# Latent attention's products split into high and low fp32r parts, with its heads prepared at other steps

## What is computed

```
proj = h @ w_in
q_g, k_g, v_g, q_lat, kv_lat = split(proj)
...
c_q = rms_norm(q_lat, mla_q_norm)
q_m = (c_q @ w_q_b).reshape(B, S, 8, 96)
q_m = concat([q_m[..., :64], apply_rope(q_m[..., 64:])])
c_kv = rms_norm(kv_lat[..., :128], mla_kv_norm)
k_rope = apply_rope(kv_lat[..., 128:])
kv = (c_kv @ w_kv_b).reshape(B, S, 8, 128)
k_m = concat([kv[..., :64], k_rope for every head])
v_m = kv[..., 64:]
o_m = blocked_attention(q_m, k_m, v_m, 96 ** -0.5)
merged = concat([rms_norm(o_g), rms_norm(o_m)])
return merged @ w_o
```

## Time and profile before

| | |
|---|---|
| median of 3 runs | 3003.57 us (3002.53 to 3005.95) |
| profiled execution, span from first to last instruction | 3003.8 us (no other time of it is shown) |
| TensorE matmul busy | 2816.4 us (94%) |
| VectorE busy | 1422.1 us (47%) |
| ScalarE busy | 1129.1 us (38%) |
| GpSimd busy | 238.4 us (8%) |
| chain that ended last | PE 82%, DVE 7%, DMA 4%, ACT 4% |

### The profile page before, as it was taken

How to read it: one execution, slowest core, us unless ns; L and a number is a source line. 1 busy time by engine, 2 the same in 40 slices (tenths; PEclk the granted TensorE clock), 3 DMA queues, 4 the chain that set the end, 5 groups by cost and what they waited for, 6 DMA issues and landing times.

```text
span 3003.8 us, 40104 instructions
## 1 busy us (share of the span) xinstructions
PE 2816.4 (94%) x16212; PEld 2094.2 (70%) x16212; DVE 1422.1 (47%) x2150; ACT 1129.1 (38%) x1920; POOL 238.4 (8%) x229
## 2 busy tenths in 40 slices
PE   7999979989999979999999789999999999799998
PEld 5657854536658745447877578888888787578886
DVE  6665532237666333244555763333334654753444
ACT  4664431124665321135233652222222542643332
POOL 0011020000011110001011010000001111000001
PEclk9999989999999989999999899999999999999999
DMA  4011249981002259993435122223320234222220
GB/s 157 29 43 59 86 173 415 415 366 64 29 29 100 100 237 418 414 395 127 144 115 153 40 76 113 112 114 128 124 84 16 88 122 130 81 84 99 98 99 28
DMA packets 67909, 428.28 MB, mean 143 GB/s; under 512 B 7968, under 2 KB 8352, under 8 KB 20368
## 3 DMA queue, kind: packets, MB, share of 16 engines
q1 hardware_dynamic: 62144, 407.96, 35.6%
q0 software_dynamic: 4432, 15.67, 1.6%
q10 hardware_dynamic: 1152, 2.10, 0.2%
HBM read 416.78 MB, written 8.91 MB: 142 GB/s over the span
## 4 chain that ended last, share of the span: by engine, by line
PE 82%; DVE 7%; DMA 4%; ACT 4%; issue 2%; POOL 2%; SPq 0%; DVEq 0%; ACTq 0%; POOLq 0%
PE banks L854 78%; PE banks L855 4%; DMA weight<-in_w_up 3%; ACT arena L1685 3%; DVE arena L2390 3%; POOL arena L3200 2%; DVE arena L3046 1%; DVE arena L2679 0%; DVE weight_part L2494 0%; DMA block_tokens_high<-df_stage 0%; DVE arena L2677 0%; DMA weight<-in_ada_w 0%; ACT weight_part L1685 0%; DVE x L2390 0%; POOL block_tokens_low L3214 0%
## 5 line engine op out<-in xcount | busy, mean ns | idle before, releaser
L1685 ACT ACTIVATE arena<-banks 128x512 f32<-128x512 f32 (+2 forms) x513 | 281.2, 550 | 885.0 <-PE banks L854 779.4
L854 PE MATMUL banks<-weight,arena 128*64 128x512 f32 (+4 forms) x2136 | 429.1, 573 | 21.3 <-DMA weight<-in_w_up 9.2
L854 PE MATMUL banks<-hidden,weight_part 128*128 128x512 f32 (+1 forms) x2304 | 446.8, 355 | 0.0
L854 PEld LDWEIGHTS banks<-hidden,weight_part 128*128 128x128 f32 x2304 | 381.2, 189 | 70.4 <-issue 3.8
L854 PE MATMUL banks<-tokens_high,weight_part 128*128 128x512 f32 (+1 forms) x1536 | 409.0, 357 | 10.0 <-ACT tokens_high L1685 10.0
L2494 DVE TENSOR_TENSOR weight_part<-weight,weight_part 128x2048 fp32r<-128x2048 f32 x124 | 285.8, 2308 | 194.8 <-ACT weight_part L1685 194.7
L1685 ACT ACTIVATE weight_part<-weight 128x2048 fp32r<-128x2048 f32 x124 | 236.4, 1908 | 349.7 <-PE banks L854 336.4
L854 PEld LDWEIGHTS banks<-weight,arena 128*64 128x64 f32 (+2 forms) x2136 | 150.9, 135 | 255.4 <-issue 233.8
L854 PEld LDWEIGHTS banks<-tokens_high,weight_part 128*128 128x128 f32 x1536 | 273.9, 190 | 62.5 <-DVE arena L2390 16.0
L3200 POOL TENSOR_TENSOR arena<-arena 128x512 f32<-128x512 f32 (+1 forms) x89 | 116.0, 1303 | 1974.3 <-ACT arena L1685 1707.4
L854 PE MATMUL banks<-tokens_low,weight_part 128*128 128x512 f32 (+1 forms) x768 | 264.7, 354 | 0.0
(11 more groups left out here) (216 smaller groups left out, 3879.6 us busy)
## 6 DMA issues: line engine op xcount, KB each, us to landing
weight<-in_w_gate SPq DMA_DIRECT2D x64, 1024.0 KB, 13.6
weight<-in_w_up SPq DMA_DIRECT2D x64, 1024.0 KB, 8.1
weight<-in_w_down SPq DMA_DIRECT2D x64, 1024.0 KB, 11.2
weight<-in_w_ff SPq DMA_DIRECT2D x64, 1024.0 KB, 4.8
weight<-in_ada_w SPq DMA_DIRECT2D x48, 1024.0 KB, 6.3
weight<-in_w_in SPq DMA_DIRECT2D x28, 1024.0 KB, 5.2
weight<-in_w_o SPq DMA_DIRECT2D x8, 1024.0 KB, 4.8
weight<-in_w_mem_kv SPq DMA_DIRECT2D x8, 1024.0 KB, 4.9
```

The costliest lines, as they stand in the source:

```text
L854: mm = lambda o, a, b, first=True, last=True: eng.matmul(o, a, b, start=first, stop=last, skip_group_check=True)
L1685: act = lambda o, i, f=ACT.Copy, **k: eng.activation(o, i, f, **k)
```

## The change

The latent attention's four kinds of products (queries, keys, values, scores) go from `tile` to `tile3`. The key products of two heads become one of 128 rows, copied raw out of its bank, then rounded and subtracted head by head; even heads hold their own 64 rows first and the rotated ones behind, odd heads the rotated rows at 32 to 63 and their own at 64 to 127, with zeros below. Keys lie in four high and four low tiles that are used twice; the rotated rows are written once. The rounded queries take places in the arena that the grouped attention has done with. `PREP_AT` becomes 10, 11, 13, 15, then 19 (heads 4 and 5) and 23 (heads 6 and 7); the values move to steps 6 to 9. `w_kv_b` is split ahead of the loop, `w_q_b` at step 6, and the `w_o` blocks at NG+1, NG+9 and NG+13 (VectorE one step later). POOL zeroes four tiles' first 32 rows, and the memory load moves behind the sixth head's cosine product. Weight columns are laid out to fit. Cut to its core (tables, column orders, arena places and renamed arguments left out; behind the step numbers come TensorE, ScalarE, VectorE and POOL, in this order):

```diff
-        is_split = lambda key: key[0] in ("w_in", "w_o", "w_mkv", "w_mq", "w_mo", "ff1", "ff2") + IN_BLOCK
+        is_split = lambda key: key[0] in ("w_in", "w_kv_b", "w_q_b", "w_o", "w_mkv", "w_mq", "w_mo", "ff1", "ff2") + IN_BLOCK
...
-        VM_AT = 4
-        PREP_AT = [NG - 4, NG - 2] + [NG + 4 * j + 2 * h for j in range(3) for h in range(2)]
+        VM_AT = 6
+        PREP_AT = {NG - 6: (0,), NG - 5: (1,), NG - 3: (2,), NG - 1: (3,), NG + 3: (4, 5), NG + 7: (6, 7)}
+        MIX_SPLITS = {6: ("w_q_b",), NG + 1: ("w_o", 0), NG + 9: ("w_o", 1), NG + 13: ("w_o", 2)}
...
+                        wcur[:] = [weight_parts(("w_q_b", l)), wcur[1]]
+                    (qh, ql), (kh, kl) = wcur
+                    at = slice(P * h, P * h + P)
+                    tile3(("qm", l, h), [(qh[:, k, at], ql[:, k, at]) for k in range(2)], [(S["CQH"][:, k, :], S["CQL"][:, k, :]) for k in range(2)],
+                          free=(WF(("w_q_b", l)),) if h == HQ - 1 else (), needs=[("cql", l, k) for k in range(2)])
+                    if h % 2 == 0:
+                        at = slice(NOPE * h, NOPE * h + P)
+                        tile3(("km", l, h // 2), [(kh[:, at], kl[:, at])], [(S["CKH"], S["CKL"])],
+                              free=(WF(("w_kv_b", l)),) if h == HQ - 2 else (), needs=[("ckvl", l)])
+                    at = slice(q * P, q * P + P)
-                        eng.wait_ge(*after(("qmr", l, h)))
-                        tile(("S", u), [S["QM"].get((l, h))[0:QK, q * P:q * P + P]], [S["KM"].get((l, h))[0:QK, :]],
-                             free=(S["QM"].free((l, h)), S["KM"].free((l, h))) if q == TB - 1 else ())
+                        eng.wait_ge(*after(("kmr", l, h % 4)))
+                        if h % 2:
+                            eng.wait_ge(*after(("zero_keys", l)))
+                        eng.wait_ge(*after(("kml", l, h)))
+                        eng.wait_ge(*after(("qml", l, h)))
+                        r = slice(0, QK if h % 2 == 0 else P)
+                        query = S["QMH"][h][r, at], S["QML"][r, h % 4, at]
+                        keys = S["KMH"][r, h % 4, :], S["KML"][r, h % 4, :]
+                        tile3(("S", u), [query], [keys], free=(S["QM"].free((l, h)), ("keys_dead", l, h)) if q == TB - 1 else ())
...
+                            wcur.append(weight_parts(("w_kv_b", l)))
+                        kh, kl = wcur[1]
+                        at = slice(c * P, c * P + P)
+                        tile3(("vm", l, c), [(S["CKH"][:, at], S["CKL"][:, at])], [(kh[:, 512:1024], kl[:, 512:1024])], needs=[("ckvl", l)])
+                    for h in PREP_AT.get(i, ()):
+                        mla_prep(h)
...
-                split_high(("w_o", l, 0))
+                split_high(("w_kv_b", l))
...
-                    m = S["KM"].take((l, h))
-                    if S["KM"].former:
-                        eng.wait_ge(*after(S["KM"].former))
-                    copy(m[0:NOPE, :], ("km", l, h), PB.get(("km", l, h))[0:NOPE, :])
-                    eng.wait_ge(*after(("ks", l)))
-                    act(m[64:96, :], S["KR"][64:96, :]).then_inc(*done(("kmr", l, h)))
-                    eng.wait_ge(scalar_step, done.count)
+                    if h % 2 == 0:
+                        raw = S["SQ"].take(("km", l, h // 2))
+                        if S["SQ"].former:
+                            eng.wait_ge(*after(S["SQ"].former))
+                        copy(raw, ("km", l, h // 2), PB.get(("km", l, h // 2)))
+                        eng.wait_ge(scalar_step, done.count)
+                        for z in (h, h + 1):
+                            if z >= 4:
+                                eng.wait_ge(*after(("keys_dead", l, z - 4)))
+                            r = nope_rows(z)
+                            act(S["KMH"][r, z % 4, :], raw[r, :]).then_inc(*done(("kmh", l, z)))
+                def mla_high(h):
+                    eng.wait_ge(*after(("qmr", l, h)))
+                    if h < 4:
+                        eng.wait_ge(*after(("out", ("S", ("g", l, h, TB - 1, 1)))))
+                    elif h == 4:
+                        eng.wait_ge(*after(("out", ("og", l, 3))))
+                    elif h == 5:
+                        for z in range(4):
+                            eng.wait_ge(*after(("kmr", l, z)))
+                    else:
+                        eng.wait_ge(*after(("keys_dead", l, h - 4)))
+                    act(S["QMH"][h], S["QM"].get((l, h))).then_inc(*done(("qmh", l, h)))
...
-                    if i in PREP_AT:
-                        mla_prep(PREP_AT.index(i))
+                    if i == 3:
+                        eng.wait_ge(*after(("ckvn", l)))
+                        act(S["CKH"], S["CKV"]).then_inc(*done(("ckvh", l)))
+                    if i == 4:
+                        for k in range(2):
+                            act(S["CQH"][:, k, :], S["CQ"][:, k, :]).then_inc(*done(("cqh", l, k)))
+                    if i == 5:
+                        eng.wait_ge(*after(("ks", l)))
+                        for z in range(4):
+                            act(S["KMH"][rope_rows(z), z, :], S["KR"][64:96, :]).then_inc(*done(("krh", l, z)))
+                    for h in PREP_AT.get(i - 2, ()):
+                        mla_high(h)
+                    for h in PREP_AT.get(i, ()):
+                        mla_prep(h)
-                    if i in (6, 10):
-                        split_high(("w_o", l, (i - 2) // 4))
+                    if i in MIX_SPLITS:
+                        split_high(mix_split(i, l))
...
-                split_low(("w_o", l, 0))
+                split_low(("w_kv_b", l))
...
+                def keys_low(h):
+                    key = ("km", l, h // 2)
+                    for z in (h, h + 1):
+                        r = nope_rows(z)
+                        eng.wait_ge(*after(("kmh", l, z)))
+                        tt(S["KML"][r, z % 4, :], S["SQ"].get(key)[r, :], S["KMH"][r, z % 4, :], SUB).then_inc(*done(("kml", l, z), *((S["SQ"].free(key),) if z % 2 else ())))
+                def mla_low(h):
+                    eng.wait_ge(*after(("qmh", l, h)))
+                    tt(S["QML"][:, h % 4, :], S["QM"].get((l, h)), S["QMH"][h], SUB).then_inc(*done(("qml", l, h)))
...
-                    if i - 1 in PREP_AT:
-                        mla_rope(PREP_AT.index(i - 1))
+                    if i == 5:
+                        eng.wait_ge(*after(("ckvh", l)))
+                        tt(S["CKL"], S["CKV"], S["CKH"], SUB).then_inc(*done(("ckvl", l)))
+                    if i == 6:
+                        for k in range(2):
+                            eng.wait_ge(*after(("cqh", l, k)))
+                            tt(S["CQL"][:, k, :], S["CQ"][:, k, :], S["CQH"][:, k, :], SUB).then_inc(*done(("cql", l, k)))
+                    if i in (8, 9):
+                        for z in (2 * i - 16, 2 * i - 15):
+                            eng.wait_ge(*after(("krh", l, z)))
+                            tt(S["KML"][rope_rows(z), z, :], K[R, :], S["KMH"][R, 0, :], SUB).then_inc(*done(("kmr", l, z)))
+                    for h in PREP_AT.get(i - 3, ()):
+                        mla_low(h)
+                    for h in PREP_AT.get(i - 1, ()):
+                        mla_rope(h)
+                        if h % 2 == 0:
+                            keys_low(h)
-                    if i in (7, 11):
-                        split_low(("w_o", l, (i - 3) // 4))
+                    if i - 1 in MIX_SPLITS:
+                        split_low(mix_split(i - 1, l))
...
+                eng.wait_ge(*after(("ks", l)))
+                for z in (1, 3):
+                    eng.memset(S["KML"][0:32, z, :].bitcast(F32), 0.0).then_inc(*done())
+                    eng.memset(S["KMH"][0:32, z, :].bitcast(F32), 0.0).then_inc(*done(*((("zero_keys", l),) if z == 3 else ())))
...
-                    if h == 2:
-                        eng.wait_ge(*after(("out", ("S", ("g", l, 3, TB - 1, 1)))))
+                    if h == 5:
+                        eng.wait_ge(*after(("out", ("S", ("m", l, 0, TB - 1, 1)))))
-                    if h == 4:
+                    if h == 5:
```

More of the change, by code:

```diff
@@ L122, in constants @@
     tabs[64:96, 2] = np.cos(am).T[np.arange(32) % 16]
-    tabs[96:112, 3] = -np.sin(am).T
-    tabs[112:128, 3] = np.sin(am).T
+    tabs[32:64, 2] = tabs[64:96, 2]
+    for b in (0, 96):
+        tabs[b:b + 16, 3] = -np.sin(am).T
+        tabs[b + 16:b + 32, 3] = np.sin(am).T
     p = np.arange(P)
@@ L165 @@
 IN_COLS = np.concatenate([np.arange(512, 640), HEAD_ROWS, np.arange(640, 1184), 1152 + SWAPPED])
-QB_COLS = np.concatenate([np.concatenate([np.arange(QK * h, QK * h + QK), QK * h + NOPE + SWAPPED]) for h in range(HQ)])
+QB_COLS = np.concatenate([np.concatenate([np.arange(QK * h, QK * h + QK), QK * h + NOPE + SWAPPED] if h % 2 == 0 else
+                                         [QK * h + NOPE + SWAPPED, np.arange(QK * h + NOPE, QK * h + QK), np.arange(QK * h, QK * h + NOPE)])
```

(27 more changed lines are left out.)

23 lines of the change are left out of this document (15 added, 8 removed).

## The result

The changed kernel takes 3014.0 us (median of 8 runs, 3007.2 to 3015.6) beside 3005.3 for the kernel before (8 runs too, 3002.5 to 3009.7): ratio 1.0023, 95% interval 1.0014 to 1.0032. The forecast was 2993.6 with a range to 3007. The profiled execution took 3014.7 us, its span is 3012.9.

The account below looks back on a forecast made before the run. TensorE's matmuls were taken to bound the mixer halves: 15.7 us saved less 10.7 lost gives 5.0 a layer, 10 in all, from 3003.6 to 2993.6 us; range 2976 to 3007.

Parts of the forecast that it names:

- What TensorE saves: Per layer, TensorE saves 9.8 us in preparation, 1.5 in values, 3.0 in scores and 1.4 in waits, sum 15.7.
- Rival 4: The three-product runs miss 0.227 us a product; at 0.39 nearly all gain is gone; chance 0.12 together with rival 3.
- The two waits of 0.7: TensorE's two waits for VectorE in the mixer halves were to go, saving 1.4 us a layer.
- Steps 5 to 7: ScalarE's rounding of rotated keys and query weight split delay scores 6 and 7: loss 1.35 us a layer.
- Steps 19 to 21: Two heads prepared at step 19, two rotations and two key lows on VectorE at step 20: loss 0.9 us.
- The estimate by the rule: VectorE and POOL exclude each other; two more meetings a layer at 1.0 us each give 2997.6 us.
- Steps 23 to 26: Head preparation, output norm, roundings and a split bunch on ScalarE and VectorE: loss 8.45 us a layer.
- The meeting with POOL that was priced at step 24: POOL's rotation product meets VectorE's second rotation at step 24, costing 0.7 us more.
- Rival 2: Clock falls in the 4.25 us gap, work behind not hidden: 2.5 us a layer lost, 2998.6 us; chance 0.16.
- its "against": Behind the gap ScalarE is late by 2.4 us anyway, which swallows the clock's loss, and the gap is shorter.
- Rival 3: VectorE in lockstep in the latent half keeps waiting for scores: 4.2 us a layer slower, 3012; chance 0.12 with rival 4.
- Rival 1: The bunched work costs nothing beyond steps 5 to 7: 14.3 us a layer gained, 2975 us; chance 0.15.

Follow-up runs that it names:

- e8_keys: Changed kernel in the spread order (heads, key lows, norm, output lows, splits over more steps), lows of heads 4 and 5 at step 20; 2979.7 us.
- e3_both: Changed kernel with the later latent heads prepared one a step and the grouped output's norm one step earlier; 2990.9 us.
- e6_pool: Changed kernel with POOL's three additions of the grouped output's squares cut from 512 to 8 columns each; 3004.6 us.
- e9_split: Changed kernel with only the split of the second output weight block moved from step 25 to 28 (VectorE 29); 3006.7 us.
- e7_filled2: Changed kernel with TensorE's waits at steps 21, 24 and 25 filled with 8, 6 and 17 plain products; 3011.2 us.
- experiment 5: The changed kernel run once more, unedited, to tell how much of its 8.7 us lies in the mixers; 3010.6 us.
- after: The changed kernel itself, without further edits, in its first measurement; 3014.0 us, ratio 1.0014 to 1.0032 to the kernel before.
- e2_norm: Changed kernel with the grouped output's norm one step earlier on ScalarE and VectorE, heads still prepared in pairs; 2998.6 us.
- e11_again: The changed kernel itself measured again, nothing edited; 3010.6 us, ratio 1.0014 to 1.0034 to the kernel before.

## Why the prediction was wrong, by its own steps

**What TensorE saves: right.** 14.3 us a layer without the two waits. The cleanest measure is e8_keys without its waits of 0.47, 0.57 and 0.39: 136.45, against 151.52 - 0.70 = 150.82 before: 14.4. The terms: a latent step is 3.50 (223.27 - 219.77), not 3.62; a step with a value product is 3.83 to 3.86 from transposes to transposes in e8_keys against 2.94 without, 0.9 and not 0.68; the preparations take 14.7 in the changed kernel and not 13.6. The errors cancel: 1.9 us a layer less, 0.9 and 1.1 more. Rival 4 is out.

**The two waits of 0.7: wrong.** They were counted as gone (1.4); 0.66 and 0.58 us are left, each behind work of VectorE on a bank, and they stay even in e8_keys. The narrower weight split couldn't take the first away: VectorE had idled 2.16 us for ScalarE ahead of the operations that end that wait, before the change and after it:

```profile
85.20 0.69 DVE L2454 SCALAR_TENSOR_TENSOR arena<-arena 128x512 f32<-128x512 f32 x1 [2.16 <-ACT arena L1719]
```

**Steps 5 to 7: right.** Forecast 1.35, measured 1.28 and 0.1 in step 7.

**Step 12: overlooked.** 0.88 us of waiting and 0.2 of slower transposes behind it: the first head's rotation and key lows, on VectorE at step 11 ahead of the maxima, were not followed at all. The key lows met POOL there, at the second head's product; what of the wait that meeting makes was not tested. VectorE, then POOL:

```profile
134.74 2.37 DVE L2641 TENSOR_TENSOR mla_key_low<-arena,mla_key_high 64x512 fp32r<-64x512 f32 x2
```

```profile
134.85 1.71 POOL L3324 TENSOR_TENSOR arena<-arena 32x512 f32<-32x512 f32 x1 [4.03 <-ACT arena L1719]
```

**Steps 19 to 21: the step that failed.** Forecast 0.9. Measured, from transposes to transposes against a latent step of 3.50: 0.47 at step 20 and 180.76 - 174.91 - 3.50 = 2.35 at step 21, then 1.3 of half clock at step 22: 4.1. I gave the two rotations and the key lows the price of VectorE alone. They met POOL twice: key lows 2.37 where they take 1.41 beside an idle POOL, as in e3_both, an addition 1.66 for 0.68, each 1.0 more. The half clock behind so short a wait stood in no term.

```profile
172.77 1.41 DVE L2641 TENSOR_TENSOR mla_key_low<-arena,mla_key_high 64x512 fp32r<-64x512 f32 x2
```

The earlier trace rows had shown such a meeting. The Trainium skill (SBUF — State Buffer, Who interferes with whom) has the two engines exclude each other in just this pairing. The trace agrees: three additions of POOL took 4.82 us, so the first ended at about 178.29, and VectorE's addition ended 0.73 behind that, near its own 0.68. The estimate by the rule, 2997.6, allowed two more meetings, 2 us a layer. The trace has three beyond the one that was priced (steps 11, 20 and 20), and e6_pool, which removes one, gives 2.3 to 2.6 us a layer, of which 1.0 is the wait and the rest the clock. The rule was weighed and then left outside the sum.

**Steps 23 to 26: near.** Forecast 1.55, 4.40 and 2.5, sum 8.45. Measured the same way: 1.8 at step 24, 4.8 at step 25 (2.84 of waiting and the half clock, as the late start of step 25 used up part of the gap), 216.28 - 208.77 - 4.38 = 3.1 at step 26 (4.38 is a step with the spread sums in e3_both): 9.8. Of the 3.1 the moved split takes away 1.7 (e9_split), so ScalarE is late there as forecast; it shows as a wait in layer 1 (1.45) and hides behind the half clock in layer 0. The meeting with POOL that was priced at step 24 came on the key lows (2.37 us) and not on the rotation. VectorE's maxima of step 24, behind the norm, began at 207.08, 16.9 after the start of step 23 (190.19); forecast 16.4.

Sum of losses: 1.4 + 1.1 + 4.1 + 9.8 = 16.4 where 10.7 were forecast, and 0.6 not regained: 6.3 of the 6.6 and 6.8 by which the mixers missed.

**Rival 2** (the clock falls and the work behind isn't hidden) had the wrong place. At the gap of step 25 its "against" held: ScalarE was late by about as much (2.65 in e7_filled2, forecast 2.4). It came true at step 21, in a wait I had put at 0.7 us, and was worth 1.3 to 1.6 where the rival had 2.5. **Rival 3** got the sign for the wrong reason: VectorE's 66 us fitted into the latent half, and it was not in lockstep (e8_keys does the same work in a mixer 16 us shorter); what failed was the order, in a few steps. **Rival 1** is what the spread order gives: 13.6 us a layer in e8_keys, near its 14.3; but this change's order is not that one.

The time lies 8.7 us above the kernel before; the mixers explain 4.7 of it, and the rest is the open part of experiment 5.

## What to carry to other kernels

When work moves to engines that are half idle, don't ask whether the sum fits; write down each engine's queue step by step, and price an instruction by a row in which its partner engine is busy, if it will be. A short wait of TensorE in mid-stream can cost more than itself: where the clock fell behind the 1.95 us at step 21, the lower clock took 1.3 to 1.6 us more. A moved step also moves the buffers that it frees: look for who takes the slot next.

## What the runs showed of the hardware

- After one and the same wait of 1.95 us in the same order of work, TensorE's granted clock fell in five layers of profiled executions (after twice, e2_norm, e9_split and e11_again in layer 1) and didn't in three (layer 0 of these last three). The Trainium skill (TensorE: Matmul & The Clock Gate, Part 1) says that the chip's watch over activity runs free of the program; the rows agree, as the order of work alone doesn't decide here. The forecast had thought of the clock only at a gap of 4 us.
- VectorE's sums and differences of two operands in the arena took 1.0 us more in each meeting with POOL that this text names (0.68 to 1.66 for one of 32 rows, 1.41 to 2.37 for two of 64), and POOL's product lost too: 1.73 us at step 20 beside the key lows, 1.26 for the product just before it (171.19).
- In a latent step the first fp32r product of a score, behind the plain float32 products of the values, took 0.34 us to the next one's start (172.93 to 173.27) and the next 0.24. Eight transposes behind a wait took 1.30 us at full clock (174.91), 1.03 without one (216.28).
